# Identity products in TensorE's waits at the second block's norms and around the last statistics of the convolution module

## The chip, the cores and the metric

The kernel runs on one core of a Trainium2 chip. The metric is the device time of one execution in microseconds. Three runs of the kernel before took 2485.75, 2487.26 and 2487.89 us; the median is 2487.26 us.

## The reference

Two transformer blocks run one after the other on 512 tokens of 1024 features, in fp32. Cut to what matters here:

```python
def first_block(x, ...):
    h = x
    h = h + mamba2_mixer(rmsnorm(h, ssm_norm), ...)
    h = h + swiglu_ffn(rmsnorm(h, ffn_norm[0]), ...)
    h = h + conformer_conv_module(rmsnorm(h, cv_norm), ...)
    h = h + swiglu_ffn(rmsnorm(h, ffn_norm[1]), ...)
    return rmsnorm(h, final_norm)

def conformer_conv_module(u, ...):
    a, g = jnp.split(u @ w_pw1 + b_pw1, 2, axis=-1)
    h = causal_depthwise_conv(a * jax.nn.sigmoid(g), dw_w, dw_b)   # 31 taps
    return jax.nn.silu(layernorm(h, ln_g, ln_b)) @ w_pw2 + b_pw2

def second_block(x, ...):
    h = modulate(rmsnorm_2(x, norm_ffn1), sh1, sc1)
    x = x + 0.5 * g1 * swiglu(h, w_ffn1_in, w_ffn1_out)
    h = modulate(rmsnorm_2(x, norm_mix), sh2, sc2)
    ...                                                # two attentions
    x = x + g2 * (merged @ w_out)
    h = modulate(rmsnorm_2(x, norm_ffn2), sh3, sc3)
    return x + 0.5 * g3 * swiglu(h, w_ffn2_in, w_ffn2_out)
```

## The kernel before

Activations lie with features on the partitions: eight tiles of 128 features by 512 tokens. Each fp32 product is made of three products of rounded parts (high and low): for one 128x128 weight tile and one activation tile, lines 528 to 530 multiply high by high, high by low and low by high, each 128x512. A linear layer adds eight such triples up in one PSUM bank. The weights come from HBM in chunks of eight tiles; ScalarE or GpSimd rounds a chunk to its high part and GpSimd subtracts to get the low part.

Each engine's program is written out by hand in the order in which it runs; the engines wait for each other by semaphores. A first pass over the program notes when each PSUM bank is let go, and the function `bank` gives out the one of the eight banks that comes free first.

**The norms.** While the last layer before a norm is produced, ScalarE squares the updated residual tile by tile and VectorE adds the squares up over the tiles (`acc`, finished after tile 6). TensorE then sums over the partitions: `token_sums` (line 546) makes 16 products with a column of ones, first for the accumulated squares, then for those of tile 7 (`sq`). ScalarE takes the root, VectorE inverts it, and TensorE spreads the per-token factors over all partitions with products of a broadcast column and the identity (`spread_halves`, line 579; `spread`, line 570), in two halves of the tokens. VectorE multiplies, ScalarE adds the modulation's shift and rounds to the high part (`XH`), VectorE makes the low part (`XL`). The next linear layer starts with four outputs at once: for tile 0 it first makes the eight products that need only `XH` (lines 517 and 518), then the four that need `XL` (line 521), and from tile 1 on the usual triples. The names in the program are s4 for the final norm of the first block (together with the first norm of the second block, hence two sums, f and f2), s5 for the norm before the mixer, and s6 for the norm before the last feed-forward.

**The convolution module.** TensorE makes the taps of the last feature tiles (line 778), then the layer norm's statistics for the tiles in the order of `LN_ORDER`, (0, 1, 3, 4, 5, 2, 6, 7): for each of the last four a run of sums for the mean and one for the squares (line 546 both times). Tile 7 waits for VectorE, which centres it, and its squares for ScalarE. Then the mean and the inverse deviation are spread (line 570, eight products), VectorE subtracts and scales (lines 2077 and 2095 for tile 0), ScalarE and VectorE make the gate, the high part and the low part (line 1482), and the second pointwise layer starts in the same early manner as at the norms.

Of the kernel before, what the change touches and what calls it, by code (L numbers as in the profile page):

```python
# [15 lines left out]
P = 128  # L16
# [167 lines left out]
class Steps:  # L184
# [9 lines left out]
    def at(self, *key):  # L194
        if self.known is None:
            return None, 0
        name, n = self.known[key]
        return self.sems[name], n
# [36 lines left out]
def build(nc, dram, steps):  # L235
    at, noted = steps.at, steps.noted
    stream = []
    with ExitStack() as ctx:
# [231 lines left out]
        def pe_program(e):  # L470
# [24 lines left out]
            def weights(tile):  # L495

                c, j = divmod(len(stream), CT)
                stream.append(tile)
                if c == 0 and j == 0:
                    w.wait_ge(*at("split", 0, "half"))  # L500
                if j == (4 if c == 0 else 0):
                    w.wait_ge(*at("split", c))
                s = c % NSPL
                return WH[:, s, j * P:(j + 1) * P], WL[:, s, j * P:(j + 1) * P], c, j == CT - 1

            def linear(keys, tiles, slots, ready, of, between=None, eager=False):


                bs = [bank(k, o) for k, o in zip(keys, of if isinstance(of, list) else [of] * len(keys))]
                for i, x in enumerate(slots):  # L510
                    if between:
                        between(i)
                    if eager and i == 0:
                        first = [weights(t[0]) for t in tiles]
                        w.wait_ge(*at("xhi", *ready(0)[1:]))
                        for b, (wh, wl, c, ends) in zip(bs, first):
                            e.matmul(b, wl, XH[:, x, :], start=True, stop=False)
                            e.matmul(b, wh, XH[:, x, :], start=False, stop=False)
                        w.wait_ge(*at(*ready(0)))
                        for b, (wh, wl, c, ends) in zip(bs, first):  # L520
                            p = e.matmul(b, wh, XL[:, x, :], start=False, stop=False)
                            if ends:
                                p.then_inc(*did(("used", c)))
                        continue
                    for key, b, t in zip(keys, bs, tiles):
                        wh, wl, c, ends = weights(t[i])
                        w.wait_ge(*at(*ready(i)))
                        e.matmul(b, wh, XH[:, x, :], start=i == 0, stop=False)  # L528
                        e.matmul(b, wh, XL[:, x, :], start=False, stop=False)  # L529
                        p = e.matmul(b, wl, XH[:, x, :], start=False, stop=i == len(slots) - 1)  # L530
                        marks = [("used", c)] if ends else []
                        if i == len(slots) - 1:
                            marks.append(("sum", *key))
                            steps.note(("chunk", *key), c)
                        if marks:
                            p.then_inc(*did(*marks))
# [4 lines left out]
            def token_sums(b, src, mat, start, stop):  # L541

                n = mat.shape[1]
                for c in range(4):
                    for q in range(0, P, 32):
                        p = e.matmul(b[q:q + 32, c * n:(c + 1) * n], src[:, c * P + q:c * P + q + 32], mat,  # L546
                                     start=start and c == 0, stop=stop and c == 3)
                return p

            def sum_of(s, of, second=False):  # L550

                b = bank((s, "f"), of)
                w.wait_ge(*at("acc", s, 6))
                token_sums(b, acc0, one, True, False)
                if second:
                    b2 = bank((s, "f2"), of)
                    w.wait_ge(*at("acc2", s, 6))
                    token_sums(b2, rs[1], one, True, False)
                w.wait_ge(*at("sq", s, 7))
                token_sums(b, tmp[3], one, False, True).then_inc(*did(("sum", s, "f")))  # L560
                if second:
                    w.wait_ge(*at("sq2", s, 7))
                    token_sums(b2, tmp[1], one, False, True).then_inc(*did(("sum", s, "f2")))

            def spread(key, v, of, n=1):

                b = bank(key, of)
                for c in range(4):
                    for g in range(n):
                        p = e.matmul(b[g * P // n:(g + 1) * P // n, c * P:(c + 1) * P],  # L570
                                     v[:, c * n + g:c * n + g + 1].broadcast_to([P, P // n]), ident, start=True, stop=True)
                p.then_inc(*did(("sum", *key)))

            def spread_halves(key, v):

                for k in range(2):
                    b = bank((*key, k), ANY)
                    for c in (2 * k, 2 * k + 1):
                        p = e.matmul(b[:, c * P:(c + 1) * P], v[:, c:c + 1].broadcast_to([P, P]), ident, start=True, stop=True)
                    p.then_inc(*did(("sum", *key, k)))  # L580
# [123 lines left out]
            def ffn(n):  # L704
# [5 lines left out]
                if n == 2:  # L710
                    final_norm()
                if n == 3:
                    sum_of("s6", ANY)
                    w.wait_ge(*at("rstd", "s6"))
                    spread_halves(("s6", "w"), small("s6"))
                linear([("gate", n, 0), ("up", n, 0), ("gate", n, 1), ("up", n, 1)], [gate(0), up(0), gate(1), up(1)], X8,
                       x_at, ANY, eager=n > 1)
                if n == 2:
# [30 lines left out]
                back(len(GROUPS) - 1)  # L749

            def final_norm():
                sum_of("s4", ANY, True)
                w.wait_ge(*at("rstd", "s4b"))
                spread_halves(("s4", "w2"), small("s4b"))

            def conformer():
                def x_at(i):
# [68 lines left out]
                    taps(7, 4 + 4 * k, 8 + 4 * k)  # L826
                taps(7, 20, 30)
                mean = bank(("mean", 1), (5,))
                for i in LN_ORDER[4:]:
                    mean_of(i)  # L830
                    squares_of(i)
                w.wait_ge(*at("mean", 1))
                spread(("mw", 1), small("mean", 1), (0,))
                w.wait_ge(*at("var"))
                bank(("t", 0), (1,))
                bank(("t", 1), (7,))
                spread(("vw", 0), small("var"), (2,))

                def y_at(i):
                    return "x", "cv", i  # L840
# [1 line left out]
                def pw2(m):  # L842
                    return column("cv_w_pw2", 0, m)
# [4 lines left out]
                    if i == NT - 1:  # L848
                        bank(("acc", "s3"), (0,))

                linear([("p2", m) for m in range(4)], [pw2(m) for m in range(4)], list(range(8, 16)), y_at, B2, acc_bank, eager=True)
                for m in range(4, NT):
                    linear([("p2", m)], [pw2(m)], list(range(8, 16)), y_at, B2)

            def mixer():
                def x_at(i):
                    return "x", "n1", i

                sum_of("s5", ANY)
                w.wait_ge(*at("rstd", "s5"))  # L860
                spread_halves(("s5", "w"), small("s5"))
                w.wait_ge(s_mix, 32)

                def tiles(n, i):
# [1510 lines left out]
```

## Time and profile before

| | |
|---|---|
| median of three runs | 2487.26 us |
| the profiled execution | 2486.98 us |
| its span, first to last instruction | 2485.2 us |
| mean granted TensorE clock | 0.989 |
| TensorE busy | 98% of the span |
| VectorE, GpSimd, ScalarE busy | 49%, 43%, 35% |

The span is the time from the first to the last instruction of the program on the core; 1.8 us of the execution lie around it. The granted clock is the share of TensorE's full speed that it was given: 1.00 is the higher level and 0.50 the lower one. Of the 25-us slices of the span, those with a mean below 1.00 lie in the first 450 us and at the four places named in the title.

### The profile page before, as it was taken

To read this page: it belongs to the slowest core of one execution; us is meant where nothing else is said; L and a number is where in the kernel's file an instruction comes from. 1 tells how busy PE (TensorE), PEld (TensorE's weight loads), DVE (VectorE), ACT (ScalarE), POOL (GpSimd) and SP (SyncE) were. 2 spreads that over 40 slices of the span, in tenths; PEclk is the share of its full clock that TensorE was granted. 3 is DMA by queue.
4 is the path that set the end of the run, shared out by engine and by line. 5 is a ranking of instruction groups with operands and counts; after the bars stand their busy time and mean duration, and the time that the engine had idled before them with its cause. 6 is when DMAs were issued, how large, how long until landed. Compare 5 with 4: busy or idle time off the path is not lost.

```text
span 2485.2 us, 31574 instructions
## 1 busy us (share of the span) xinstructions
PE 2437.0 (98%) x13071; PEld 1976.6 (80%) x13071; DVE 1224.5 (49%) x2008; ACT 864.6 (35%) x1357; POOL 1078.5 (43%) x502
## 2 busy tenths in 40 slices
PE   8999999999999998999999999999999999999999
PEld 6778887888888877888887888887766678788887
DVE  7777667553444886553435632115465544322222
ACT  3434544122223415122223232223566742222221
POOL 4344345544444453644444554443322234544443
PEclk9999999999999998999999999999999999999999
DMA  4112223554442221554422233232211122223232
GB/s 159 52 60 79 75 70 108 172 176 156 167 136 93 94 86 60 187 179 152 152 94 94 82 107 102 93 102 77 77 60 52 60 77 93 85 94 101 93 102 85
DMA packets 72286, 257.42 MB, mean 104 GB/s; under 512 B 8144, under 2 KB 8656, under 8 KB 72144
## 3 DMA queue, kind: packets, MB, share of 16 engines
q1 hardware_dynamic: 60048, 214.98, 26.8%
q10 hardware_dynamic: 12096, 40.42, 4.5%
q8 instruction: 103, 1.69, 0.3%
q14 instruction: 39, 0.32, 0.0%
HBM read 253.28 MB, written 2.10 MB: 103 GB/s over the span
## 4 chain that ended last, share of the span: by engine, by line
PE 89%; DVE 8%; ACT 2%; issue 1%; ACTq 0%; POOL 0%; DVEq 0%
PE ps L528 27%; PE ps L529 27%; PE ps L530 27%; PE ps L778 2%; DVE tmpm L1473 1%; DVE arena L1473 1%; PE ps L585 1%; DVE XL L1482 1%; PE ps L570 1%; PE ps L546 1%; PE ps L940 1%; PE ps L873 1%; PE ps L930 1%; PE ps L683 1%; PE ps L919 0%
## 5 line engine op out<-in xcount | busy, mean ns | idle before, releaser
L2261 POOL TENSOR_TENSOR WL<-raw,WH 128x1024 fp32r<-128x1024 f32 x400 | 972.6, 2434 | 1137.1 <-ACT WH L980 1129.3
L528 PE MATMUL ps<-XH,WH 128*128 128x512 f32 x3144 | 1237.1, 393 | 11.5 <-DVE XL L1473 8.2
L529 PE MATMUL ps<-XL,WH 128*128 128x512 f32 x3144 | 1226.9, 390 | 0.0
L530 PE MATMUL ps<-XH,WL 128*128 128x512 f32 x3144 | 1226.6, 390 | 0.0
L528 PEld LDWEIGHTS ps<-XH,WH 128*128 128x128 f32 x3144 | 592.8, 189 | 145.7 <-issue 8.4
L530 PEld LDWEIGHTS ps<-XH,WL 128*128 128x128 f32 x3144 | 592.2, 188 | 124.3
L529 PEld LDWEIGHTS ps<-XL,WH 128*128 128x128 f32 x3144 | 592.7, 189 | 123.3 <-issue 2.2
L980 ACT ACTIVATE WH<-raw 128x1024 fp32r<-128x1024 f32 x302 | 318.3, 1057 | 725.0 <-PE ps L530 605.0
L1473 DVE SCALAR_TENSOR_TENSOR arena<-arena,ps 128x512 f32<-128x512 f32 x88 | 60.4, 687 | 514.2 <-ACT arena L1183 503.8
L2259 POOL CAST WH<-raw 128x1024 fp32r<-128x1024 f32 x98 | 106.6, 1087 | 247.9 <-PE ps L530 203.6
L1473 DVE SCALAR_TENSOR_TENSOR h<-ps,der,h 128x512 f32<-128x512 f32 (+1 forms) x106 | 77.7, 740 | 176.7 <-PE ps L530 176.7
L1547 DVE TENSOR_TENSOR h<-h,ps 128x512 f32<-128x512 f32 x127 | 84.7, 684 | 105.4 <-PE ps L530 105.1
L1187 ACT ACTIVATE XH<-ps 128x512 fp32r<-128x512 f32 x88 | 52.8, 600 | 177.7 <-DVE ps L1829 92.1
L1791 DVE CUSTOM_DVE_ANT_0 arena<-arena 128x1024 f32<-128x1024 f32 x72 | 96.1, 1372 | 0.0
L1482 DVE TENSOR_TENSOR XL<-ps,XH 128x512 fp32r<-128x512 f32 x92 | 63.6, 692 | 62.5 <-ACT XH L1187 58.6
L1183 ACT ACTIVATE arena<-ps 128x512 f32<-128x512 f32 x88 | 51.5, 586 | 66.1 <-DVE ps L1821 51.6
L1473 DVE SCALAR_TENSOR_TENSOR arena<-ps,vec,arena 128x512 f32<-128x512 f32 (+29 forms) x95 | 64.8, 728 | 0.8
L1473 DVE SCALAR_TENSOR_TENSOR tmpm<-ps,der,tmpm 128x509 f32<-128x509 f32 (+2 forms) x72 | 53.9, 749 | 22.1 <-ACT tmpm L1061 20.4
L1821 DVE TENSOR_TENSOR ps<-ps,rsm 128x512 f32<-128x512 f32 x44 | 30.5, 694 | 37.7 <-PE ps L530 34.0
L1001 ACT ACTIVATE tmpm<-h 128x512 f32<-128x512 f32 x46 | 28.7, 623 | 43.7 <-DVE h L1473 34.8
L1473 DVE SCALAR_TENSOR_TENSOR XL<-h,vec,XH 128x512 fp32r<-128x512 f32 x32 | 39.9, 1248 | 6.2 <-ACT XH L990 6.2
L1080 ACT ACTIVATE arena<-ps,arena 128x128 f32<-128x128 f32 x128 | 36.5, 372 | 15.0 <-PE ps L617 15.0
(276 smaller groups left out, 1713.7 us busy)
## 6 DMA issues: line engine op xcount, KB each, us to landing
raw<-in_w SPq DMA_DIRECT2D x403, 512.0 KB, 3.4
arena<-in_w_mod ACTq DMA_DIRECT2D x72, 512.0 KB, 3.7
o_out<-h SPq DMA_DIRECT2D x8, 256.0 KB, 2.0
h<-in_x SPq DMA_DIRECT2D x4, 256.0 KB, 7.6
h<-in_x ACTq DMA_DIRECT2D x4, 256.0 KB, 6.3
raw<-in_w SPq DMA_DIRECT2D x2, 256.0 KB, 4.2
arena<-in_c ACTq DMA_DIRECT2D x1, 512.0 KB, 4.4
vec<-in_vec ACTq DMA_DIRECT2D x1, 295.5 KB, 9.4
```

The lines of the kernel that those rows point to most:

```text
L528: e.matmul(b, wh, XH[:, x, :], start=i == 0, stop=False)
L529: e.matmul(b, wh, XL[:, x, :], start=False, stop=False)
L530: p = e.matmul(b, wl, XH[:, x, :], start=False, stop=i == len(slots) - 1)
L980: A(WH[:, c % NSPL, :], raw[:, c % NRAW, :], ACT.Copy).then_inc(*did(("hi", c)))
L1183: A(t, ps("gate", n, j), ACT.Tanh, scale=0.5).then_inc(*did(("ft", n, j)))
L1187: A(XH[:, 8 + 4 * (g % 2) + i, :], ps("up", n, j), ACT.Copy).then_inc(*did(("xhi", "a", n, j)))
L1473: return e.scalar_tensor_tensor(out=out, in0=a, scalar=s, in1=b, op0=op0, op1=op1)
L1482: TT(XL[:, slot, :], src, XH[:, slot, :].bitcast(F32), SUB).then_inc(*did(("x", *key), *free))
L1547: TT(h[:, m, :], h[:, m, :], ps(*key), ADD).then_inc(*marks)
L1791: e.tensor_tensor_reduce(out=t, in0=t, in1=crow, scale=1.0, scalar=0.0, op0=MUL, op1=ADD, accum_out=modv[:, i:i + 1]).then_inc(*did(("mod" ...
L2259: e.tensor_copy(hi, x).then_inc(*did(("hi", c)))
L2261: e.tensor_tensor(lo, x, hi.bitcast(F32), SUB).then_inc(*did(("split", c)))
```

## The change

TensorE multiplies the identity by the identity, 128x128 in fp32, into a PSUM bank that it holds already and overwrites later, at places where its program has a wait ahead. A new function `keep_on` does it:

```diff
+            def keep_on(b, n):
+                for _ in range(n):
+                    e.matmul(b[:, 0:P], ident, ident, start=True, stop=True)
```

The three norms of the second block go through one function. It takes the banks for the spread values first, before the sums' bank, and puts four identity products before the wait for the squares of tile 7 and three before the wait for the inverse:

```diff
-            def sum_of(s, of, second=False):
+            def sum_of(s, of, second=False, idle=None):
...
+                if idle is not None:
+                    keep_on(idle, 4)
                 w.wait_ge(*at("sq", s, 7))
...
-            def spread_halves(key, v):
-
-                for k in range(2):
-                    b = bank((*key, k), ANY)
+            def sum_and_spread(s, key, v, rstd, second=False):
+
+
+                bs = [bank((*key, k), ANY) for k in range(2)]
+                sum_of(s, ANY, second, bs[0])
+                keep_on(bs[0], 3)
+                w.wait_ge(*at("rstd", rstd))
+                for k, b in enumerate(bs):
                     for c in (2 * k, 2 * k + 1):
                         p = e.matmul(b[:, c * P:(c + 1) * P], v[:, c:c + 1].broadcast_to([P, P]), ident, start=True, stop=True)
                     p.then_inc(*did(("sum", *key, k)))
```

A linear layer that starts early gets five more before its wait for the first high part, eleven in the convolution module:

```diff
-            def linear(keys, tiles, slots, ready, of, between=None, eager=False):
+            def linear(keys, tiles, slots, ready, of, between=None, eager=False, idle=5):
...
                         first = [weights(t[0]) for t in tiles]
+                        keep_on(bs[0], idle)
                         w.wait_ge(*at("xhi", *ready(0)[1:]))
```

And in the convolution module, around the statistics of tile 7 (`spread` is given its bank here, so that the products can go into it first):

```diff
-                for i in LN_ORDER[4:]:
+                for i in LN_ORDER[4:7]:
                     mean_of(i)
                     squares_of(i)
+                keep_on(banks[0], 6)
+                mean_of(7)
+                keep_on(banks[0], 2)
+                squares_of(7)
+                b = bank(("mw", 1), (0,))
+                keep_on(b, 3)
                 w.wait_ge(*at("mean", 1))
-                spread(("mw", 1), small("mean", 1), (0,))
-                w.wait_ge(*at("var"))
+                spread(("mw", 1), small("mean", 1), None, b=b)
                 bank(("t", 0), (1,))
                 bank(("t", 1), (7,))
-                spread(("vw", 0), small("var"), (2,))
+                b = bank(("vw", 0), (2,))
+                keep_on(b, 1)
+                w.wait_ge(*at("var"))
+                spread(("vw", 0), small("var"), None, b=b)
```

Added in all: 12 identity products at each of the three norms, 23 in the convolution module. Nothing is taken away, and the other engines' programs stay as they are.

## Rows read from the trace of the kernel before

**Rows 1.** The page: busy times, instruction queue, shares of the chain that ended last.

```profile
PE 2437.0 (98%) x13071; PEld 1976.6 (80%) x13071; DVE 1224.5 (49%) x2008; ACT 864.6 (35%) x1357; POOL 1078.5 (43%) x502
...
q8 instruction: 103, 1.69, 0.3%
...
PE 89%; DVE 8%; ACT 2%; issue 1%; ACTq 0%; POOL 0%; DVEq 0%
```

**Rows 2.** Windows: length, busy us (instructions) of each engine, granted clock, DMA share, GB/s.

```profile
937.80:951.40 13.60, 9.88 (x92) 8.32 (x92) 9.19 (x22) 7.34 (x13) 0.00 (x0) 0.50 0.13 41
1357.70:1367.80 10.10, 8.01 (x47) 6.45 (x38) 7.74 (x19) 4.39 (x8) 1.17 (x1) 0.50 0.17 54
1729.70:1733.00 3.30, 3.09 (x7) 2.48 (x8) 3.23 (x7) 1.51 (x3) 0.00 (x0) 0.50 0.03 5
2118.90:2125.60 6.70, 5.56 (x13) 4.43 (x14) 6.56 (x15) 3.85 (x6) 0.00 (x0) 0.50 0.21 78
```

**Rows 3.** Timeline (start, us, instruction, [idle before <-releaser]): big products at either clock.

```profile
1354.19 0.39 PE L530 MATMUL ps<-XH,WL 128*128 128x512 f32 x1
...
1354.87 0.39 PE L530 MATMUL ps<-XH,WL 128*128 128x512 f32 x1
...
1731.33 0.63 PE L518 MATMUL ps<-XH,WH 128*128 128x512 f32 x1
...
1732.18 0.63 PE L518 MATMUL ps<-XH,WH 128*128 128x512 f32 x1
```

**Rows 4.** Timeline of the norm before the mixer (s5).

```profile
1724.70 0.39 PE L530 MATMUL ps<-XH,WL 128*128 128x512 f32 x1
...
1726.51 0.43 PE L546 MATMUL ps<-cst,tmpm 128*32 128x1 f32 x32 [1.05 <-ACT tmpm L999]
...
1727.54 0.97 PEld L579 LDWEIGHTS ps<-cst,smallm 128*128 128x128 f32 x8 [0.69 <-DVE smallm L1525]
...
1729.91 0.77 PE L517 MATMUL ps<-XH,WL 128*128 128x512 f32 x1 [1.21 <-ACT XH L1246]
...
1731.49 0.74 DVE L1473 SCALAR_TENSOR_TENSOR XL<-tmpm,modv,XH 128x512 fp32r<-128x512 f32 x1
```

**Rows 5.** Timeline of the final norm of the first block (s4).

```profile
1356.86 0.43 PE L546 MATMUL ps<-cst,tmpm 128*32 128x1 f32 x32 [0.71 <-ACT tmpm L999]
...
1357.47 0.53 PE L546 MATMUL ps<-cst,tmpm 128*32 128x1 f32 x32 [0.18 <-ACT tmpm L1006]
...
1358.88 1.78 PEld L579 LDWEIGHTS ps<-cst,smallm 128*128 128x128 f32 x8 [0.97 <-DVE smallm L1888]
...
1362.16 0.77 PE L517 MATMUL ps<-XH,WL 128*128 128x512 f32 x1 [1.21 <-ACT XH L1246]
```

**Rows 6.** Timeline of the norm before the last feed-forward (s6).

```profile
2116.63 0.43 PE L546 MATMUL ps<-cst,tmpm 128*32 128x1 f32 x32 [1.06 <-ACT tmpm L999]
...
2120.04 0.76 PE L517 MATMUL ps<-XH,WL 128*128 128x512 f32 x1 [1.21 <-ACT XH L1246]
```

**Rows 7.** Timeline of the convolution module's last statistics and the layer behind.

```profile
933.45 0.40 PE L778 MATMUL ps<-XH,WL 64*128 64x512 f32 x2
...
936.78 0.26 PE L546 MATMUL ps<-cst,arena 128*32 128x1 f32 x10 [1.56 <-issue]
...
938.77 0.61 PE L546 MATMUL ps<-cst,arena 128*32 128x1 f32 x32 [1.45 <-DVE arena L2038]
...
939.97 3.48 PEld L570 LDWEIGHTS ps<-cst,smallm 128*128 128x128 f32 x16
...
943.79 0.75 DVE L2095 TENSOR_TENSOR arena<-arena,ps 128x256 f32<-128x256 f32 x2 [1.02 <-PE ps L570]
...
946.45 0.76 PE L517 MATMUL ps<-XH,WL 128*128 128x512 f32 x1 [2.70 <-ACT XH L1328]
...
951.87 0.19 PEld L528 LDWEIGHTS ps<-XH,WH 128*128 128x128 f32 x1 [0.69 <-DVE XL L1482]
...
953.83 0.69 DVE L1482 TENSOR_TENSOR XL<-arena,XH 128x512 fp32r<-128x512 f32 x1 [0.21 <-ACT XH L1320]
```

More of the change, by code:

```diff
@@ L563, in sum_of, with spread @@
                     token_sums(b2, tmp[1], one, False, True).then_inc(*did(("sum", s, "f2")))
-            def spread(key, v, of, n=1):
-                b = bank(key, of)
+            def spread(key, v, of, n=1, b=None):
+                b = bank(key, of) if b is None else b
                 for c in range(4):
@@ L712, in ffn @@
                 if n == 3:
-                    sum_of("s6", ANY)
-                    w.wait_ge(*at("rstd", "s6"))
-                    spread_halves(("s6", "w"), small("s6"))
+                    sum_and_spread("s6", ("s6", "w"), small("s6"), "s6")
                 linear([("gate", n, 0), ("up", n, 0), ("gate", n, 1), ("up", n, 1)], [gate(0), up(0), gate(1), up(1)], X8,
@@ L751, in final_norm @@
             def final_norm():
-                sum_of("s4", ANY, True)
-                w.wait_ge(*at("rstd", "s4b"))
-                spread_halves(("s4", "w2"), small("s4b"))
+                sum_and_spread("s4", ("s4", "w2"), small("s4b"), "s4b", True)
             def conformer():
@@ L849, in acc_bank @@
                         bank(("acc", "s3"), (0,))
-                linear([("p2", m) for m in range(4)], [pw2(m) for m in range(4)], list(range(8, 16)), y_at, B2, acc_bank, eager=True)
+                linear([("p2", m) for m in range(4)], [pw2(m) for m in range(4)], list(range(8, 16)), y_at, B2, acc_bank, eager=True, idle=11)
                 for m in range(4, NT):
@@ L857, in x_at @@
                     return "x", "n1", i
-                sum_of("s5", ANY)
-                w.wait_ge(*at("rstd", "s5"))
-                spread_halves(("s5", "w"), small("s5"))
+                sum_and_spread("s5", ("s5", "w"), small("s5"), "s5")
                 w.wait_ge(s_mix, 32)
```

## The prediction

> **What bounds the kernel now.** I read the page first: its busy shares and its chain that ended last say TensorE, busy 98% of the span and 89% of the chain [rows 1]. A change that adds work to TensorE can therefore only pay where TensorE waits, or by what it does to TensorE's speed. Next, the granted clock, by stretches: at the four places of the change it reads 0.50, the lower level (1.2 GHz), for 13.6, 10.1, 3.3 and 6.7 us [rows 2], against 1.00 (2.4 GHz) in the dense work around them. Third, what a level is worth, from the timeline. At full clock three products of 128x512 take 0.68 us (1354.19 to 1354.87), 0.227 each; at 0.50 two take 0.85 (1731.33 to 1732.18), 0.425 each [rows 3]. Every big product issued at 0.50 costs 0.2 us more. The reader is to see that the short idle times at the norms cost little by themselves; the low clock that follows them, when the real products are already running, costs more.
>
> **Unit cost of what is added.** One identity product is an fp32 product of 128x128, the same shape as those of the spreading lines, which appear as two load-and-multiply pairs per product. The eight pairs (four products) before the mixer take 0.97 us of loads at full clock [rows 4]: 0.24 us a product, or 0.22 without the tail of the last load; I take 0.225. At 0.50, 16 pairs take 3.48 us [rows 7]: 0.43 a product. No wait is added; banks are only asked for earlier. At each norm the banks now taken first are the two for the spread values, and the sum gets the third or fourth to come free. With eight banks in turn and some 2.7 us for each output block before, those have long been read; I cost the permutation at nothing, with up to 0.1 us per norm for the range.
>
> **Norm before the mixer (s5).** Four, three and five identity products go into waits of 1.05 us, 0.69 and 1.21 us [rows 4]. They need 0.90, 0.67 and 1.12 us, so all fit, the second by a hair (0 to 0.1 us of delay). TensorE is then almost never quiet between the last dense product and the first new one at 1729.91, so I expect the clock not to fall. Real products ran at 0.50 from 1729.91 to 1733.1: 3.2 / 0.425 = 7.5 products, which at full clock take 1.7 us. Gain 1.5 us. What is late next is the low part of tile 1: VectorE finishes it at 1731.49 + 0.74 = 1732.23, and TensorE wants it at 1729.91 + 12 x 0.227 = 1732.63. Covered.
>
> **Norm before the last feed-forward (s6).** Same layout; the first wait is 1.06 us [rows 6]. Products ran low from 2120.04 to 2125.6: 5.6 / 0.425 = 13.2, at full clock 3.0 us. Gain 2.6 us.
>
> **Final norm of the first block (s4).** The first wait is 0.71 us, the four identity products need 0.90, so the sums of 1356.86 start 0.1 to 0.2 us late; but the sums after them wait for ScalarE until 1357.47 anyway, so nothing is lost [rows 5]. Those last sums run in 0.43 instead of 0.53 us: gain 0.1. The spread takes 1.78 us of loads at 0.50 against 0.97 in rows 4; from its start to the first big product went 3.28 us here [rows 5], 2.37 us at s5 [rows 4]: gain 0.9. Products ran low from 1362.16 to 1367.8: 5.65 / 0.425 = 13.3, at full clock 3.0: gain 2.65. Together 3.65 us. The three norms give 1.5 + 2.6 + 3.65 = 7.75 us.
>
> **Convolution statistics.** This is the place that decides. The last tap product starts at 933.45 and is over by about 933.85. Then come only one-column sums, and in the middle of one run of them TensorE stands 1.56 us with no releaser, until 936.78 [rows 7]. Nothing was waited for; the fetch of its own instructions is the likeliest reason (the instruction queue moves them in 103 blocks of about 16 KB [rows 1], and these sums use them up fastest). The change puts its first identity product behind these sums, at about 937.2, so the quiet stretch of 3.4 us stays. How soon the clock fell after the end of the dense work can be read three times: 2.6 us at s4 (1355.1 to 1357.7), 4.8 at s5 (1724.9 to 1729.7) and here 3.95 (937.8) [rows 2 to 4, 7]. Added to 933.85 this gives 936.4 to 938.6, mostly before or shortly after the first identity product. So I expect the clock to fall here still, at about 937.8.
>
> Then the added products run at 0.43 us and lie in front of the real work. Six from 937.2: 2.5 at full clock, 3.5 x 0.43 = 1.5 us, end 939.3; the mean sums started at 938.77 before (+0.5). Sums 0.53, end 939.8; two more products, 940.7; square sums 0.53, end 941.2; three products, 942.5; first spread, 8 pairs x 0.215 = 1.7, end 944.2; one product, 944.6. When does the clock come back? At s5 it came back 3.2 us, at s4 and s6 5.6 us, and in this stage 5.0 us after big products started; the 3.78 us of spreading did not bring it back [rows 2, 4 to 7]. With sparse sums among the products I take 944.6 (bounds 941 and the 951.4 of before). The second spread then takes 0.9 us and VectorE's scaling starts at about 945.7 instead of 943.79 [rows 7]: +1.9 us. Everything behind hangs on that VectorE chain: it delivers one tile each 2.7 us (tile 1 at 951.82, released at 951.87; tile 2 at 953.83 + 0.69 [rows 7]), as long as TensorE's 12 products at full clock (12 x 0.227 = 2.72), so 1.9 us late stays 1.9 us late.
>
> And a faster clock opens a new wait. In the kernel before, the first 12 products ran at 0.50 and filled the time until tile 1 (946.45 to 951.87, with 0.69 idle) [rows 7]. At full clock they are done in 2.7 us and TensorE is quiet for 5.42 - 2.72 = 2.7 us, with no identity products there. A quiet stretch of that size can drop the clock again; a second stretch like that of s5 (3.3 us, 7.8 products at 0.425, each 0.2 late) costs 1.6 us, and TensorE can't make that up, as its pace equals VectorE's. I count it. The convolution place: +1.9 + 1.6 = **+3.5 us**. If the clock never fell there, the same sums done at full clock give scaling at 942.85: -0.95. The eleven products before the first big product (2.5 us) fit into the 2.66 us that VectorE and ScalarE need.
>
> **Sum.** 2486.98 us (span 2485.2 and 1.8 around it) - 7.75 + 3.5 = 2482.7. The median of the runs shown is 0.3 above the profiled execution, which I leave as noise.
>
> By itself, and needed by nothing above: the Trainium skill, "TensorE: Matmul & The Clock Gate", Part 1, says that the moment of a clock change varies from run to run of the same kernel. The rows agree as far as one profile can: three nearly equal norms stayed low for 3.3, 6.7 and 10.1 us. By that rule the 7.75 is one draw; three times the middle norm would be 7.8, so the sum hardly moves by it.
>
> **Rivals.**
> (a) The clock holds at the convolution, because the identity products arrive in time. For it: it has fallen up to 4.8 us after dense work (s5), and the first identity product comes after 3.4. Against it: two of the three falls that I could time came within 4 us. It gives 2486.98 - 7.75 - 0.95 = 2478.3, or about 2480 where a norm would have lost less. Chance 0.27.
> (b) Forecast's convolution, but norms that were worth less than in the profiled execution: with s5's 1.5 us plus s4's 0.9 for its spread, each norm is worth 1.5, together 3 x 1.5 + 0.9 = 5.4, hence 2485.1. Chance 0.15.
> (c) On the other side: the identity products don't hold the clock. For it: 16 such pairs in a row at the convolution started and ended at 0.50 [rows 7]. Against it: big products too needed up to 5.6 us, and their streaming at 0.11 us a pair leaves no holes. Price, if the clock falls wherever it fell before: at the convolution all runs at 0.43, the second spread ends at 946.35, the eleven products take 4.7 us and end at 951.05, 4.6 us later than 946.45; at s4 three products end at 1359.3 (+0.4) and five more push the first product to 1363.2, +1.05 in all; at s6 four of the five run low, +0.55; s5 fits. Sum +6.2: 2493.2, slower. It decides only if TensorE gets no credit for these products in at least the convolution and s4. Chance 0.08.
> The Trainium skill has a rule on this side, same page, Part 4: multiplications by the identity in transpose mode don't engage the full clock. Applied to this change it would give the 2493.2 of (c). These are plain fp32 products; no row here has a long run of either kind alone at full clock.
>
> **How the numbers follow.** Forecast 0.50, its own range 2481 to 2485.5: the second fall of the clock at the convolution may be missing (-1.6), or the norms may be worth 2 us less. (a) 0.27, (b) 0.15, (c) 0.08. The range of 8 in 10 takes in the forecast, (b) and most of (a): 2479.0 to 2486.2. About 0.2%, 5 us, is what a measurement of this kernel can tell from no change; the bound lies at 2482.3, close to the forecast. Faster by over that: (a) and a quarter of the forecast, 0.40. Slower: most of (c), 0.06. Within: 0.54.
>
> **What would show it.** At the three norms of the second block: granted clock 1.00 throughout, identity rows in the waits, first big product within 0.1 us of its old distance (s4: 0.9 to 1.0 us shorter). At the convolution: the 1.56 us hole still there, a low stretch that begins near 937.8 and ends before 945, the scaling after 945, and an idle time of 2 to 3 us ahead of tile 1. If the clock reads 1.00 there, (a) holds; if it still reads 0.50 at s4 and s6, (c). The prediction is wrong if banks taken early make the sums wait, or if the added instructions open new holes without a releaser.

## The result

| | before | after |
|---|---|---|
| median | 2486.59 us (14 runs, 2484.45 to 2488.35) | 2481.55 us (14 runs, 2480.08 to 2483.14) |
| profiled execution, span | 2485.2 us | 2480.7 us |
| mean granted clock | 0.989 | 0.994 |

The ratio is 0.9979, 95% interval 0.9972 to 0.9986: 5.0 us faster, against a forecast of 4.6 us below the median then shown (2482.7 us). More runs moved the median of the kernel before from 2487.26 to 2486.59 us. The gain is clear of zero, and its 0.20% is just the size that the prediction took as the least that can be told from no change.

The page of the kernel after answers to [rows 1]: TensorE does a little more work in a shorter span.

```profile
PE 2443.7 (99%) x13189; PEld 1985.1 (80%) x13189; DVE 1218.0 (49%) x2008; ACT 864.5 (35%) x1357; POOL 1079.4 (44%) x502
...
q8 instruction: 104, 1.70, 0.3%
...
PE 91%; DVE 7%; ACT 2%; issue 0%; ACTq 0%; DVEq 0%
```

To see where the time went, one can take the first product of the sums at each of the four places as a milestone. The timeline of the kernel before:

```profile
933.78 0.43 PE L546 MATMUL ps<-cst,arena 128*32 128x1 f32 x32
...
1355.21 0.43 PE L546 MATMUL ps<-cst,summ 128*32 128x1 f32 x32
...
1725.02 0.43 PE L546 MATMUL ps<-cst,summ 128*32 128x1 f32 x32
...
2115.15 0.43 PE L546 MATMUL ps<-cst,summ 128*32 128x1 f32 x32
```

and of the kernel after (the function of line 546 has moved to 547):

```profile
934.12 0.43 PE L547 MATMUL ps<-cst,arena 128*32 128x1 f32 x32
...
1358.70 0.43 PE L547 MATMUL ps<-cst,summ 128*32 128x1 f32 x32
...
1724.76 0.43 PE L547 MATMUL ps<-cst,summ 128*32 128x1 f32 x32
...
2113.27 0.43 PE L547 MATMUL ps<-cst,summ 128*32 128x1 f32 x32
```

| from ... to | before | after | difference | forecast |
|---|---|---|---|---|
| start, convolution statistics | 933.78 | 934.12 | +0.34 | 0 |
| convolution statistics, s4 | 421.43 | 424.58 | +3.15 | +3.5 |
| s4, s5 | 369.81 | 366.06 | -3.75 | -3.65 |
| s5, s6 | 390.13 | 388.51 | -1.62 | -1.5 |
| s6, end of the span | 370.05 | 367.43 | -2.62 | -2.6 |
| sum | | | -4.50 | -4.25 |

The first row is not the change's work: up to there the program is the same, and over the profiled executions of the kernels below this distance lies between 932.21 and 935.63 us. The three rows of the norms repeat: in every execution below with the first seven or all twelve identity products at the norms, and no stop inside them, they are 366.06 to 366.11, 388.46 to 388.67 and 367.34 to 367.45 us. Without the products they vary: they add up to 1130.0 us in the kernel before and to 1128.5 in the one other such trace (368.41, 391.12 and 368.93, the convolution's products alone), against 1122.0 with them. So the products are worth 8.0 us against the first and 6.5 against the second.

Windows of the kernel after (columns as in [rows 2]) show the same in the clock, the column before the DMA share: low twice at the convolution, full at the three norms.

```profile
938.30:945.00 6.70, 6.70 (x90) 6.22 (x89) 1.39 (x6) 2.41 (x4) 0.00 (x0) 0.50 0.23 81
945.20:951.80 6.60, 6.45 (x46) 5.67 (x44) 5.80 (x13) 2.80 (x6) 0.00 (x0) 1.00 0.00 0
955.40:958.70 3.30, 3.30 (x9) 2.63 (x8) 3.09 (x6) 2.65 (x5) 0.00 (x0) 0.50 0.00 0
1357.70:1367.80 10.10, 9.99 (x179) 8.40 (x178) 7.54 (x20) 4.56 (x10) 3.41 (x2) 1.00 0.31 107
1727.00:1737.00 10.00, 10.00 (x56) 8.54 (x56) 8.97 (x19) 4.60 (x8) 0.00 (x0) 1.00 0.03 9
2118.00:2128.00 10.00, 10.00 (x45) 8.20 (x45) 9.82 (x17) 4.37 (x7) 3.78 (x2) 1.00 0.13 50
```

The timeline of the convolution place in the kernel after, which answers to [rows 7] (L555 are the identity products, each two pairs of load and product):

```profile
937.11 0.26 PE L547 MATMUL ps<-cst,arena 128*32 128x1 f32 x10 [1.55 <-issue]
...
937.58 2.33 PE L555 MATMUL ps<-cst 128*128 128x128 f32 x12
939.84 0.61 PE L547 MATMUL ps<-cst,arena 128*32 128x1 f32 x32
940.38 1.22 PE L555 MATMUL ps<-cst 128*128 128x128 f32 x4
941.53 0.61 PE L547 MATMUL ps<-cst,tmpm 128*32 128x1 f32 x32
942.07 1.65 PE L555 MATMUL ps<-cst 128*128 128x128 f32 x6
943.50 1.81 PE L579 MATMUL ps<-cst,smallm 128*128 128x128 f32 x8
945.15 0.39 PE L555 MATMUL ps<-cst 128*128 128x128 f32 x2
945.38 1.06 PE L579 MATMUL ps<-cst,smallm 128*128 128x128 f32 x8
...
954.56 0.50 PE L529 MATMUL ps<-XH,WH 128*128 128x512 f32 x1 [2.49 <-DVE XL L1497]
```

The hole (the idle time for which the trace shows no releaser) is there, TensorE is then busy without a break, but with identity products in front of the real work and at half clock; and TensorE waits 2.49 us for tile 1, where it waited 0.69 before.

### The profile page after: what moved, and what is told of

Read it like the earlier page. It is cut to its first block, busy times and chain, and to the rows that moved or that the text cites. A ratio compares the mean times of both kernels' runs of the same rounds, so it can differ in the third digit from the quotient of the medians.

```text
span 2480.7 us, 31810 instructions
## 1 busy us (share of the span) xinstructions
PE 2443.7 (99%) x13189; PEld 1985.1 (80%) x13189; DVE 1218.0 (49%) x2008; ACT 864.5 (35%) x1357; POOL 1079.4 (44%) x502
## 4 chain that ended last, share of the span: by engine, by line
PE 91%; DVE 7%; ACT 2%; issue 0%; ACTq 0%; DVEq 0%
PE ps L529 27%; PE ps L530 27%; PE ps L531 27%; PE ps L787 2%; DVE tmpm L1488 1%; DVE arena L1488 1%; PE ps L598 1%; PE ps L579 1%; DVE XL L1497 1%; PE ps L547 1%; PE ps L555 1%; PE ps L955 1%; PE ps L888 1%; PE ps L945 1%; PE ps L696 1%
```

## The experiments

Each ratio is to the kernel before. "Norms alone" and the like name the kernels below. The distance from the first sums to VectorE's scaling of tile 0 is used as a ruler of the convolution place: 943.79 - 933.78 = 10.01 us in the kernel before, 946.47 - 934.12 = 12.35 in the full change.

**The two halves.** First the norms alone:

```diff
-                keep_on(banks[0], 6)
                 mean_of(7)
-                keep_on(banks[0], 2)
                 squares_of(7)
                 b = bank(("mw", 1), (0,))
-                keep_on(b, 3)
...
-                keep_on(b, 1)
...
-                linear([("p2", m) ...], acc_bank, eager=True, idle=11)
+                linear([("p2", m) ...], acc_bank, eager=True, idle=0)
```

> The norms' 36 identity products are kept, the 23 of the convolution module are taken out. My theory (the norms give 6 to 7.75 us, the convolution part costs 2 to 3.5): 6 to 7.5 us faster than the kernel before, so about 2479.6 us and some 1.5 us faster than the full change; granted clock 1.00 at all three norms, and at the convolution a low stretch of 10 to 14 us as before. Rival (the convolution part is itself a gain and the norms gave less): 4 us faster than before, 2482.6 us.

Measured: 2479.66 us, ratio 0.9972 (0.9960 to 0.9983), 7.3 us faster than before and 1.9 us faster than the full change (2.3 when each is set against the runs of the kernel before that were taken beside it). The intervals of the two ratios overlap; of the single runs, only four of the full change's 14 lie below the slowest of these six. The hole is longer here, and the ruler says 10.01 us all the same (the scaling is shown further below):

```profile
938.47 0.26 PE L547 MATMUL ps<-cst,arena 128*32 128x1 f32 x10 [2.58 <-issue]
```

Then the convolution module's products alone (4, 3 and 5 taken out at the norms):

```diff
-                    keep_on(idle, 4)
+                    keep_on(idle, 0)
...
-                keep_on(bs[0], 3)
...
-            def linear(..., eager=False, idle=5):
+            def linear(..., eager=False, idle=0):
```

> Only the convolution module's 23 identity products; none at the norms. My theory: 1 to 3.5 us slower than the kernel before, about 2488.5 us; the clock falls near 938, comes back near 945, falls again after the first twelve big products; scaling of tile 0 about 2 us later than before. Rival: 1 us faster than before, 2485.6 us.

Measured: 2487.45 us, ratio 1.0002 (0.9993 to 1.0011). Scaling of tile 0, from the two timelines:

```profile
944.47 0.75 DVE L2106 TENSOR_TENSOR arena<-arena,ps 128x256 f32<-128x256 f32 x2 [1.02 <-PE ps L579]
```

```profile
947.99 0.75 DVE L2109 TENSOR_TENSOR arena<-arena,ps 128x256 f32<-128x256 f32 x2 [0.52 <-PE ps L579]
```

With the first sums at 934.46 and 935.63 these are 10.01 us (norms alone) and 12.36 us (convolution alone). The delay of 2.35 us belongs to the convolution's products. From these first sums to those of s4 the two traces with the products take 424.58 and 424.61 us, the one with the norms alone 421.39. In the median the products cost 0.5 us on top of the kernel before (inside the interval) and 1.9 on top of the norms; my bound of 1 to 3.5 was too high for the first. The halves give -7.3 + 0.5 = -6.8, and both together -5.0; the 1.8 us between are less than the executions of one kernel differ by (2485.34 to 2490.49 us here, and the profiled one was the slowest). That the convolution part is a gain, the rival, is spoken against by the full change being slower than the norms alone; the interval here would by itself still allow a gain of 1.7 us. This kernel also takes the banks at the norms in the new order, and gained nothing by it: the order of the banks is not what pays.

**Closing the quiet stretch at the convolution.** Twelve products between the six runs of sums, in place of six behind them:

```diff
+                b = bank(("mw", 1), (0,))
                 for i in LN_ORDER[4:7]:
                     mean_of(i)
+                    keep_on(b, 2)
                     squares_of(i)
-                keep_on(banks[0], 6)
+                    keep_on(b, 2)
```

> The full change, but the six identity products that stood behind the sums of tiles 5, 2 and 6 are replaced by twelve that stand between these six runs of sums, two after each. My theory (the clock falls because TensorE is quiet for 3.4 us behind the taps, and it stands without a releaser because the sums use up instructions faster than they are fetched): the idle time of 1.56 us without a releaser is gone, the clock reads 1.00 until tile 1's wait at least, scaling of tile 0 starts about 3 us earlier than in the full change; 2 to 4 us faster than the full change, about 2479 us. Rival (the clock falls there for another reason): a low stretch from about 938 stays, time within 1 us of the full change.

Measured: 2479.55 us, ratio 0.9971 (0.9960 to 0.9981), 2.0 us faster than the full change and no faster than the norms alone. No idle time without a releaser, and granted clock 1.00 through the place, also behind the wait for tile 1 (2.51 us). The scaling, though, comes 10.41 us after the first sums (933.46 to 943.87), 1.9 earlier than in the full change and not 3:

```profile
939.49 0.43 PE L547 MATMUL ps<-cst,arena 128*32 128x1 f32 x32
...
943.87 0.75 DVE L2111 TENSOR_TENSOR arena<-arena,ps 128x256 f32<-128x256 f32 x2 [0.43 <-PE ps L579]
```

One run of sums and two products take 1.01 us together (933.46 to 934.47), where I had reckoned 0.36 + 0.45: the change between the two kinds costs about 0.1 us each way. So tile 7's sums, whose input was ready about 5.0 us after the first sums, start after 6.0. Then the second quiet stretch filled as well, with products that add zero:

```diff
+                    if eager and i == 1:
+                        for _ in range(fill):
+                            e.matmul(bs[0][:, 0:P], xp[7][:, 0:1].broadcast_to([P, P]), ident, start=False, stop=False)
```

> As the run before with twelve products between the sums, and in addition ten products of a column of zeros with the identity, added into the running sum of the first output (they add zero), between the first twelve big products and tile 1 of the second pointwise layer. My theory (the second quiet stretch of 2.7 us is a second cause of low clock): granted clock 1.00 through the whole convolution place, 0 to 1.6 us faster than the run without them, about 2478.3 us. Rival (the second quiet stretch is harmless once the first is closed): same time as without, clock 1.00 in both.

Measured: 2479.48 us, ratio 0.9970 (0.9959 to 0.9982), the same as without. Its trace has clock 1.00 throughout, but so had the one before it, in which the wait for tile 1 stayed open: there was no second low stretch to close in that execution. And the hole is back, later in the stream, at a place where the trace before, whose stream is the same up to there, has none; the scaling comes 12.08 us after the first sums (932.42 to 944.50):

```profile
939.45 0.38 PE L550 MATMUL ps<-cst,tmpm 128*32 128x1 f32 x25
941.35 0.24 PE L550 MATMUL ps<-cst,tmpm 128*32 128x1 f32 x7 [1.51 <-issue]
```

**What the hole is.** Next the products in three groups, none in front of tile 7's work:

```diff
-                for i in LN_ORDER[4:7]:
+                b = bank(("mw", 1), (0,))
+                for i, n in zip(LN_ORDER[4:7], (4, 4, 2)):
                     mean_of(i)
                     squares_of(i)
-                keep_on(banks[0], 6)
+                    keep_on(b, n)
                 mean_of(7)
-                keep_on(banks[0], 2)
                 squares_of(7)
-                b = bank(("mw", 1), (0,))
-                keep_on(b, 3)
...
-                keep_on(b, 1)
```

> The norms' identity products are kept. In the convolution module ten identity products stand in three groups (4, 4 and 2) behind the sums of tiles 5, 2 and 6, and none from tile 7's sums on (they lay in front of real work); the eleven before the first big product are kept. My theory (two costs of the convolution part: low clock after a quiet stretch, and products in front of work whose inputs are ready): no idle time without a releaser, granted clock 1.00, scaling of tile 0 about 8.2 us after the first sums, against 10.0 in the kernel before and 12.3 in the full change; 1.5 to 2 us faster than with the norms alone, about 2477.7 us. Rival (what remains there is bound by something else, since the norms alone, the products between the sums, and those with the second gap filled all took 2479.5 us): 2479.5 us again.

Measured: 2481.49 us (2478.39 to 2484.31 in 11 runs), ratio 0.9978 (0.9970 to 0.9987): a miss. The profiled execution was the 2478.39 one; there the scaling comes 8.48 us after the first sums (933.90 to 942.38), 8.2 expected, with no hole and clock 1.00 up to 951.6. The other executions lie at 2479.91 us and above. So the same kernel was profiled once more:

> The version with ten products in three groups once more, unchanged, for a second look at its trace. My theory: in this execution TensorE stands without a releaser for 0.5 to 2.5 us at about the start of the first spread, and the time is above 2480 us. Rival: no such idle time, and the second low stretch as in the first look.

Measured: 2484.01 us, and there is the hole, at the head of the first spread (16 pairs: 1 and 15), with the clock at 0.50 for 3.2 us from 942.07 on:

```profile
940.63 0.38 PE L579 MATMUL ps<-cst,smallm 128*128 128x128 f32 x1
942.20 3.49 PE L579 MATMUL ps<-cst,smallm 128*128 128x128 f32 x15 [1.19 <-issue]
...
1359.10 0.67 PE L547 MATMUL ps<-cst,tmpm 128*32 128x1 f32 x55
1361.57 0.25 PE L547 MATMUL ps<-cst,tmpm 128*32 128x1 f32 x9 [1.80 <-issue]
```

A second one stands in s4's sums, in a place where neither the kernel before nor the full change has one; the clock fell to 0.50 there too (1361.9 to 1365.3), and from s4's first sums to those of s5 it is 369.17 us in place of 366.07.

Count pairs from the first sums of the convolution place. Kernel before: 4 x 32 + 22 = 150 pairs, then the hole; all seven traces with this stream (the kernel before, the full change, both halves, and three below) have it there, 1.55 to 2.58 us long. Filled version: 7 x 32 + 25 of sums and 14 products of two pairs, 277. Here: 8 x 32 + 10 products x 2 + 1, 277. The place at 277 lies 127 pairs, 254 instructions, behind the one at 150, and the page has 103 instruction blocks for 2 x 13071 instructions, 254 a block. So holes sit at block ends, and only where the block before was used up fast: in 1.1 to 3.3 us by the timelines, where a block of big products lasts 127 x 0.227 = 29 us. From 900 us on, no trace has a stop of over 0.2 us without a releaser anywhere else. Whether there is one at 277, and how long it is, differs between executions. That cause is shown by position, not by seeing the fetch itself. The next run moves the position:

```diff
-                taps(7, 20, 30)
                 mean = bank(("mean", 1), (5,))
+                keep_on(mean, 8)
+                taps(7, 20, 30)
```

> As the norms alone, with eight identity products (32 instructions, 16 pairs of load and product) put before the last taps. My theory (the idle time without a releaser comes at a fixed place of TensorE's instruction stream, where a fetched block ends): it moves from behind the 22nd of the 32 pairs of tile 6's mean sums to behind the 6th. Rival (it is tied to the data or to VectorE): it stays behind the 22nd.

Measured: 2480.58 us in one execution. The hole is neither behind the 22nd nor behind the 6th pair of that run of sums; it is gone, and TensorE waits for VectorE's tile 7 without a break from the sixth run of sums on:

```profile
940.29 0.58 PE L547 MATMUL ps<-cst,arena 128*32 128x1 f32 x32 [3.17 <-DVE arena L2050]
```

and the window from the fall of the clock on:

```profile
940.40:954.10 13.70, 10.93 (x94) 8.86 (x93) 9.49 (x22) 7.74 (x14) 0.00 (x0) 0.50 0.09 34
```

Neither theory had that. "Tied to the data or to VectorE" would have kept the hole; mine would have moved it. My guess is that the fetch, too, was asked for earlier, during the slow taps; no run tests it, and as it is one execution, chance is not excluded (at 277 the hole was there in two executions of four). Two things it does show. The quiet stretch before tile 7 stays and the clock falls all the same, at 940.4 for 13.7 us, so the hole is not needed for the fall. And the scaling comes 10.01 us after the first sums (935.29 to 945.30), as with holes of 1.56 and 2.58 us: at its old place the hole itself cost nothing. Now fewer instructions for the same streaming:

```diff
+            def keep_on_wide(b, n):
+                for _ in range(n):
+                    e.matmul(blocks4(b), ident, ident.unsqueeze(1).broadcast_to([P, 4, P]), start=True, stop=True)
...
-                for i, n in zip(LN_ORDER[4:7], (4, 4, 2)):
+                for i in LN_ORDER[4:7]:
                     mean_of(i)
                     squares_of(i)
-                    keep_on(b, n)
+                    keep_on_wide(b, 1)
```

> As the version with ten identity products in three groups behind the sums of tiles 5, 2 and 6, but each group is one product of the identity with four copies of it side by side, 128x512: about the same streaming (12 for 10) with 12 instructions in place of 40. Its profiled execution was its fastest and the others lay 3 us above it. My theory (in most executions of that version TensorE runs out of fetched instructions at the start of the first spread, where a block of 256 instructions ends; with 28 fewer ahead the end of the block lies behind the second spread, where nothing waits for it): 2478.3 us, and a smaller spread of the runs. Rival (the instruction count has no part in it; the loss is the clock falling in the second quiet stretch): as before, 2481.5 us.

Measured: 2477.73 us (2477.03 to 2479.21 in 7 runs), ratio 0.9968 (0.9957 to 0.9979). This is the fastest median: 3.8 us below the full change, with the three groups' 5.9 us spread of runs down to 2.2. No hole at the convolution place in its trace; scaling 8.55 us after the first sums (932.21 to 940.76); low clock only behind the wait for tile 1:

```profile
940.76 0.75 DVE L2111 TENSOR_TENSOR arena<-arena,ps 128x256 f32<-128x256 f32 x2 [0.64 <-PE ps L583]
...
948.85 0.19 PEld L529 LDWEIGHTS ps<-XH,WH 128*128 128x128 f32 x1 [2.91 <-DVE XL L1498]
```

```profile
932.00:949.50 17.50, 14.68 (x319) 10.71 (x316) 14.07 (x26) 8.99 (x16) 3.39 (x2) 1.00 0.15 48
949.70:952.90 3.20, 3.20 (x9) 2.52 (x8) 2.99 (x6) 2.55 (x5) 0.00 (x0) 0.50 0.00 0
```

The second low stretch is still there, so it is not what cost the three groups their 3.8 us, as the rival had it. How much of the 1.9 us below the norms alone the convolution place gave is open: in the two traces the four distances from its first sums to the end add up to 1543.1 us here and 1543.3 there.

The last step fills that wait with two wide products that add zero (the `fill` edit above, with the wide operand):

> As the run with three wide products, and in addition two wide products of a column of zeros with four copies of the identity, which add zero to the first output, between the first twelve big products and tile 1. My theory: this closes the second quiet stretch, clock 1.00 through the whole place in every execution, scaling of tile 0 about 8.5 us after the first sums, 2477 us. Rival (instruction count has no part, only the second quiet stretch): 2477 us too, but then the run without these two stays at 2481.5.

Measured: 2480.42 us, ratio 0.9974 (0.9964 to 0.9983): 2.7 us slower than without, against both theories. In its trace the convolution place is clean, clock 1.00; but s4, 400 us later, has a hole amid the identity products, and the clock fell there at 1356.4:

```profile
1354.90 0.38 PE L558 MATMUL ps<-cst 128*128 128x128 f32 x1
1356.02 1.11 PE L558 MATMUL ps<-cst 128*128 128x128 f32 x5 [0.74 <-issue]
1356.93 1.92 PE L599 MATMUL ps<-cst,smallm 128*128 128x128 f32 x8
```

The run without the fill has a hole of 0.28 us at the end of the same six pairs and keeps the clock. The fill is eight instructions, and the hole at s4 lies four pairs, eight instructions, earlier. The second execution of the three groups fits too: it has 14 pairs more ahead than the run without the fill, and its hole at s4 lies 14 pairs earlier (nine sums and five identity pairs). So in three different streams the hole stands behind the same number of pairs, some 2290 from the convolution's first sums: position decides, over 400 us behind the edit. The fill itself did its work: from the convolution's first sums to s4's it is 419.63 us, 420.82 without; s4 then takes 368.15 in place of 366.31. In the two profiled executions that is 1.1 us slower in all (2478.21 and 2477.09); that it makes the whole 2.7 of the medians is argued, from one trace each.

**Which products matter at the norms.** From the norms alone, either the last five only or the first seven only:

```diff
-                    keep_on(idle, 4)
+                    keep_on(idle, 0)
...
-                keep_on(bs[0], 3)
```

> As the norms alone, but only the five products before the first big product; the four and the three around the sums are taken out. My theory (the clock falls for the quiet time before the spread): it still falls at some of the three norms, most likely at s4; a half of the gain, 3 to 4 us faster than the kernel before, about 2483.5 us. Rival (the last wait of 1.21 us is what drops the clock): clock 1.00 at all three, 2479.7 us as with all twelve.

```diff
-            def linear(..., eager=False, idle=5):
+            def linear(..., eager=False, idle=0):
```

> As the norms alone, but only the four and the three products around the sums; the five before the first big product are taken out. My theory: clock 1.00 at all three norms, nearly the whole gain, 2480 us. Rival (the last wait drops the clock): clock low from about the first big product on at some norms, 2483 us or more.

Measured: the last five 2483.59 us, ratio 0.9985 (0.9976 to 0.9995); the first seven 2479.15 us, ratio 0.9969 (0.9958 to 0.9981). The first seven bring all of the 7.3 us; the last five alone bring half, 3.7. Windows of the last five at s4, s5 and s6; in this execution the clock held at s6, which the expectation left open, and of the norms' distances only the last is as with all twelve (368.53, 389.83 and 367.40 us):

```profile
1357.90:1364.50 6.60, 5.72 (x39) 5.34 (x32) 4.43 (x12) 2.76 (x6) 1.09 (x1) 0.50 0.25 81
1726.60:1729.70 3.10, 3.10 (x15) 3.10 (x16) 1.68 (x5) 1.01 (x2) 0.00 (x0) 0.50 0.03 5
2112.00:2122.00 10.00, 8.34 (x105) 6.83 (x104) 6.01 (x14) 3.55 (x8) 3.38 (x2) 1.00 0.32 105
```

and of the first seven at all three norms, where TensorE again has the wait of about 1.2 us before the first big product:

```profile
1352.00:1364.00 12.00, 10.68 (x177) 8.79 (x177) 9.40 (x23) 6.02 (x12) 3.41 (x3) 1.00 0.28 91
1722.00:1732.00 10.00, 8.79 (x46) 7.38 (x45) 8.88 (x19) 4.69 (x8) 0.00 (x0) 1.00 0.02 7
2112.00:2122.00 10.00, 8.79 (x40) 7.18 (x40) 9.82 (x20) 4.82 (x8) 2.88 (x3) 1.00 0.14 54
```

**Busy, but streaming nothing.** From the norms alone, each identity product becomes two products of the identity with one column:

```diff
-                for _ in range(n):
-                    e.matmul(b[:, 0:P], ident, ident, start=True, stop=True)
+                for _ in range(2 * n):
+                    e.matmul(b[:, 0:1], ident, one, start=True, stop=True)
```

> As the norms alone, but every identity product is replaced by two products of the identity with a single column: TensorE has an instruction under way in the waits, yet streams next to nothing. My theory (the clock follows how much TensorE really streams): the clock falls at the norms as in the kernel before, nothing is gained, 2486.5 us. Rival (it is enough that TensorE is not idle): clock 1.00, 2479.7 us.

Measured: 2502.04 us, ratio 1.0061 (1.0048 to 1.0074). The clock fell as expected; the size is a miss. TensorE is busy in every microsecond of these windows at s4 and s6, and the clock is low in all of them:

```profile
1358.10:1371.60 13.50, 13.50 (x115) 12.70 (x116) 8.67 (x22) 4.40 (x9) 1.05 (x1) 0.50 0.12 41
2129.50:2139.60 10.10, 10.10 (x40) 9.23 (x40) 8.30 (x17) 4.28 (x7) 0.00 (x0) 0.50 0.16 52
```

```profile
1356.36 2.09 PE L555 MATMUL ps<-cst 128*128 128x1 f32 x16
1358.38 1.03 PE L547 MATMUL ps<-cst,tmpm 128*32 128x1 f32 x64
```

A one-column pair takes 2.02 / 16 = 0.126 us at the higher level, no less than the 0.11 of a pair of 128 columns, so two for one doubled the time, overran each wait and delayed the norms: the spread at s4 starts 6.43 us behind the first sums (1355.49 to 1361.92), 3.67 before, and the distances of the three norms are 4.5, 5.6 and 4.4 us longer than in the kernel before. The mechanism that I priced as a rival at 2493.2 us (products that outlast the waits without holding the clock) exists; the identity products don't suffer from it, these do.

## Why the prediction was right

**The bound and the unit prices** held. The identity pair ran at 0.11 us and 0.21 us at the two clocks (22 pairs 2.62 and 10 pairs 1.28; 6 pairs 1.65 and 4 pairs 1.22); the eleven before the first big product took 2.62 us for the 2.5 reckoned.

**The three norms** were the part that carried the result: 7.75 us forecast, 3.75 + 1.62 + 2.62 = 8.0 in the profiled execution, 7.3 as the median of the norms alone. The causal step, that streaming in the waits keeps the clock up, is shown by taking it apart: seven products hold it and bring the gain, twice as many with one column do not. At s4 the sums after the first four products started 0.3 us late (1.96 us behind the first sums, 1.65 before), twice what I had reckoned, and it cost nothing, as written: the spread began 3.60 us behind the first sums, 3.67 before. What I had not seen is that only the first seven products matter; the five before the first big product, which I had counted in, add nothing that could be measured (2479.66 against 2479.15 us).

**The banks** taken earlier made no sum wait: the first sums at s4, s5 and s6 start 0.34, 0.32 and 0.32 us behind the start of the last big product, as before.

**The convolution place** went as written, step by step: hole still there (1.55 us), clock low from 938.3 (937.8 forecast) to 945.1 (944.6), scaling 2.35 us late (1.9), a new wait of 2.49 us for tile 1 (2.7), a second low stretch of 3.4 us. Forecast +3.5, measured +3.15 in the profiled execution. As a median over executions the term is too large: 1.9 us between the norms alone and the full change. A likely reason is that I had treated one profile's timing of the clock as if it were every execution's; the second low stretch, at 1.6 us, is the term in doubt. Six profiled executions have the wait of 2.46 to 2.51 us for tile 1, and the clock fell behind it in four (full change, convolution alone, three groups, wide) and held in two (twelve products between the sums, three groups again). Beside it stands what the Trainium skill says in "TensorE: Matmul & The Clock Gate", Part 1, that the moment of a clock change varies from run to run of the same kernel; the traces of the three groups agree, as the clock fell at 951.6 behind a wait of 2.50 us in the first execution and stayed at 1.00 behind one of 2.51 in the second.

**The rivals.** (a), the clock holds at the convolution, did not happen in the two profiles with these products (full change, convolution alone). (b), norms worth 5.4 us, has the 7.3 of the median against it, and the 8.0 and 6.5 by which the norms' distances shrank against the two traces without the products; the interval of the norms alone, 4.2 to 9.9 us, would still allow it. (c) is excluded by the clock of 1.00 at the norms. Its row, 16 pairs that started and ended at 0.50, was not evidence that identity products don't count: big products too needed several microseconds to bring the clock back. The Trainium skill's rule on transpose mode ("TensorE: Matmul & The Clock Gate", Part 4), cited there, stays untested: no run here put transposes into a wait. The forecast sat 0.4 us from the 0.2% bound, and the measured ratio of 0.9979 sits on it; which side it would be, the traces could not say.

**The sum** was closer than its parts deserve: 7.3 for 7.75, 1.9 for 3.5, and the median before 0.7 us lower than the three runs shown. The norms were put 0.4 us too high and the convolution 1.6, errors that cancel in part; that is luck.

## What to carry to other kernels

Filling TensorE's waits with real streaming pays when the fill ends before the awaited input arrives, and it belongs where the quiet begins, not just ahead of the heavy work: seven products behind the sums gave all of 7.3 us, five ahead of the big products gave half. Never put fill in front of work whose input is ready, above all where the clock may already be low and the fill itself runs at half speed. Where many tiny instructions run, count instructions as well as time: fill with few wide products (12 instructions for 40 gave 3.8 us over the three groups of small ones, in the median), and expect that an edit in one place moves block ends and holes everywhere behind it.

## What the runs showed that was not expected

- TensorE stops for 0.3 to 2.6 us at ends of instruction blocks of about 254 instructions, in some executions, when a block is used up in 1.1 to 3.3 us; the same kernel has the stop in one execution and not in the next (2478.39 and 2484.01 us).
- A product with one moving column costs no less (0.126 us a pair) than one with 128 (0.11), in fp32 with 128 weight columns; 9.8 us of such products, sums and the spread (1358.10 to 1367.89), TensorE busy all the time, stood at 0.50.
- Changing between runs of small sums and identity products costs about 0.1 us each way, so twelve products in six places took about 1 us more than their own time.
- Filling the convolution's waits brought little even where it kept the clock up: against the norms alone, the median with twelve products between the sums is 0.1 us lower (0.2 with the last wait filled too), with three small groups 1.8 higher, with three wide products 1.9 lower and, with the last wait filled too, 0.8 higher.
